# The softmax attention stage of a two-block network: a narrower wait before the differential scores, transposes ahead of the scores in local units, share arithmetic ahead of the maxima

## The reference, cut to what matters

```python
# differential attention, 4 heads, values 128 wide, all 1024+256 keys
s1 = einsum('bqhd,bkhd->bhqk', q1, k1) * SCALE
s2 = einsum('bqhd,bkhd->bhqk', q2, k2) * SCALE
w = softmax(s1) - lam * softmax(s2)
out = einsum('bhqk,bkhe->bqhe', w, v)
# local attention with a sink, 8 heads (2 key heads), values 64 wide,
# a band of 3*128 keys (masked by |q - k| <= 128) and 256 context keys
p = softmax(concat([where(valid, s, -1e30), sink]))[..., :-1]
out = einsum('bhgqk,bkhd->bqhgd', p, v)
```

## Time and profile before

| | us |
|---|---|
| median of 3 runs | 3744.65 (3729.24 to 3747.63) |
| the profiled execution, its time | 3722.19 |
| its span, first to last instruction | 3720.2 |
| TensorE busy, share of the span | 3367.1, 91% |
| mean granted TensorE clock, share of 2.4 GHz | 0.957 |
| pairs of D and L, from the first D's scores to the last D's | 590.28 to 997.44 |

### The profile page before, as it was taken

One profiled execution on the slowest core, in us unless ns is written; L12 is line 12 of the kernel. 1 busy time (PEld: TensorE's weight loads), 2 busy tenths in 40 slices (PEclk: granted clock), 3 DMA queues, 4 the chain that ended last, 5 costly groups with the idle time before them and its releaser, 6 DMA issues. The chain is left out here.

```text
span 3720.2 us, 52552 instructions
## 1 busy us (share of the span) xinstructions
PE 3367.1 (91%) x21754; PEld 2892.5 (78%) x21754; DVE 1628.5 (44%) x2517; ACT 1226.3 (33%) x2230; POOL 260.4 (7%) x332
## 2 busy tenths in 40 slices
PE   7899978999878999997989998887888899999988
PEld 2699976666667999875878995556776799999777
DVE  2306725555555112166536204553555445554343
ACT  3212325555564234223534103442332211111232
POOL 2000000000011000011211100001110000000010
PEclk9899988999988999998999998998999899999999
DMA  9224550000063222233321212001003211111332
GB/s 330 85 83 149 158 181 29 12 12 12 7 214 127 77 73 75 80 115 135 111 51 36 86 44 62 13 1 7 2 2 109 68 45 45 45 45 56 107 126 95
DMA packets 196721, 289.30 MB, mean 78 GB/s; under 512 B 41606, under 2 KB 137670, under 8 KB 194480
## 3 DMA queue, kind: packets, MB, share of 16 engines
q1 hardware_dynamic: 176624, 216.90, 18.1%
q0 software_dynamic: 19904, 69.65, 5.8%
HBM read 217.60 MB, written 68.90 MB: 77 GB/s over the span
## 5 line engine op out<-in xcount | busy, mean ns | idle before, releaser
L115 PE MATMUL p_pb<-p_w_hi,h_hi 128*128 128x416 f32 (+2 forms) x1216 | 425.0, 350 | 6.7 <-DVE p_w_lo L110 6.7
L117 PE MATMUL p_pb<-p_w_hi,h_lo 128*128 128x416 f32 (+2 forms) x1216 | 422.2, 347 | 0.0
L116 PE MATMUL p_pb<-p_w_lo,h_hi 128*128 128x416 f32 (+2 forms) x1216 | 420.0, 345 | 0.0
L115 PE MATMUL fu_pf<-h_hi,fu_w_hi 128*128 128x344 f32 (+1 forms) x1056 | 339.8, 322 | 8.7 <-DVE fu_pf L3426 8.7
L116 PE MATMUL fu_pf<-h_lo,fu_w_hi 128*128 128x344 f32 (+1 forms) x1056 | 340.6, 323 | 0.0
L117 PE MATMUL fu_pf<-h_hi,fu_w_lo 128*128 128x344 f32 (+1 forms) x1056 | 339.2, 321 | 0.0
L115 PEld LDWEIGHTS p_pb<-p_w_hi,h_hi 128*128 128x128 f32 x1216 | 229.2, 189 | 15.7 <-issue 14.4
L116 PEld LDWEIGHTS p_pb<-p_w_lo,h_hi 128*128 128x128 f32 x1216 | 229.4, 189 | 1.9
L117 PEld LDWEIGHTS p_pb<-p_w_hi,h_lo 128*128 128x128 f32 x1216 | 229.2, 188 | 0.6
L115 PEld LDWEIGHTS fu_pf<-h_hi,fu_w_hi 128*128 128x128 f32 x1056 | 200.1, 190 | 9.0 <-DVE fu_pf L3426 9.0
L117 PEld LDWEIGHTS fu_pf<-h_hi,fu_w_lo 128*128 128x128 f32 x1056 | 200.0, 189 | 0.0
(11 more groups left out here) (521 smaller groups left out, 7162.5 us busy)
## 6 DMA issues: line engine op xcount, KB each, us to landing
mod_w<-in_adaln_w SPq DMA_DIRECT2D x12, 2048.0 KB, 16.3
fu_raw<-in_ffn_up SPq DMA_DIRECT2D x88, 256.0 KB, 3.1
fd_raw<-in_ffn_down SPq DMA_DIRECT2D x44, 512.0 KB, 3.6
la_qkv<-p SPq DMA_DIRECT2D x16, 1024.0 KB, 5.1
p<-p_o SPq DMA_DIRECT2D x60, 208.0 KB, 1.9
s_raw<-in_w_in POOLq DMA_DIRECT2D x48, 256.0 KB, 3.5
rT<-p_stage SPq DMA_DIRECT2D x10, 896.0 KB, 4.8
p_raw<-in_ab_w_in POOLq DMA_DIRECT2D x10, 832.0 KB, 6.5
```

The source lines that it names most:

```text
L115: pe.matmul(out, left[0], right[0], start=start, stop=False)
L116: pe.matmul(out, left[0], right[1], start=False, stop=False)
L117: return pe.matmul(out, left[1], right[0], start=False, stop=stop)
```

## The change

Three edits, all in `attention_even`.

1. D's first scores after an L wait for `expd` to reach n - 1, so for L's first exponential alone; a new wait for n stands ahead of D's second scores. The first D, which follows a context unit, keeps its wait for n there.
2. In an L step TensorE transposes the first four blocks of unit u-2 (and waits for its weights) before L's first scores instead of after them. In a D step the order stays.
3. The reciprocal and the share of a `da` or `dac` unit move out of `finish` into `shares`, which VectorE runs for unit u-1 after `take(u-3)` and before `maxima(u)`. It has the wait for both exponentials of u-1 that `finish` has. The combination stays in `finish`.

No instruction of arithmetic is added or removed, and no DMA is touched; SyncE's and GpSimd's programs are the same.

```diff
+                def shares(u):
+                    s, n, h = u % 2, exps_before[u], 4 if units[u][0] == "dac" else 1
+                    dve.wait_ge(expd, n + 2)
+                    dve.reciprocal(r[u % 4][:, 0:2 * h], l[s][:, 0:2 * h]).then_inc(recips, 1)
+                    dve.wait_ge(recips, u + 1)
+                    dve.scalar_tensor_tensor(ratio[:, 0:h], l[s][:, 0:h], g.neglam[:, :], r[u % 4][:, h:2 * h],
+                                             ALU.mult, ALU.mult).then_inc(ratioed, 1)
...
                     if kind in ("da", "dac"):
                         h = 4 if kind == "dac" else 1
                         k = joins_before[u]
-                        dve.reciprocal(r[u % 4][:, 0:2 * h], l[s][:, 0:2 * h]).then_inc(recips, 1)
-                        dve.wait_ge(recips, u + 1)
-                        dve.scalar_tensor_tensor(ratio[:, 0:h], l[s][:, 0:h], g.neglam[:, :], r[u % 4][:, h:2 * h],
-                                                 ALU.mult, ALU.mult).then_inc(ratioed, 1)
                         dve.wait_ge(ratioed, k + 1)
...
                     if u >= 3:
                         take(u - 3)
+                    if 1 <= u <= NU and units[u - 1][0] in ("da", "dac"):
+                        shares(u - 1)
                     if u < NU:
                         maxima(u)
...
                     n = exps_before[u]
+                    near_before = u and kind in ("da", "wa") and units[u - 1][0] in ("da", "wa")
                     if u and part == 0:
-                        pe.wait_ge(expd, n - 1 if kind == "wa" and units[u - 1][0] == "da" else n)
+                        pe.wait_ge(expd, n - 1 if near_before else n)
+                    if near_before and kind == "da" and part == 1:
+                        pe.wait_ge(expd, n)
...
+                    windowed = u < NU and units[u][0] == "wa"
+                    if u < NU and not windowed:
                         score(u, 0)
                     if u >= 2:
                         weighed(u - 2)
                         turn(u - 2, 0)
+                    if windowed:
+                        score(u, 0)
                     if u < NU:
                         score(u, 1)
```

## The result

The changed kernel takes 3687.59 us (median of 4 runs, 3674.2 to 3698.48), the kernel before 3736.94 (4 runs, 3729.21 to 3747.63). The ratio is 0.987, 95% interval 0.9842 to 0.9899: about 49 us, or 1.3%, faster, with 38 to 59 us inside the interval. Eleven more runs of the kernel before, taken later, had a median of 3728.93 us; against those the gain is 41 us. Much of the spread between runs goes with the granted clock: at a mean of 0.951 the kernel before took 3742.62 us and the changed one 3698.48, at 0.953 3739.56 and 3687.24, at 0.954 3733.33 to 3734.34 and 3687.95, so at like clocks 44 to 52 us lie between them. The forecast was 3706 us with a range down to 3694, so the time fell outside it, on the fast side.

The account below looks back on a forecast made before the run. TensorE, busy 91% of the span, was taken as the bound; 31 x 0.76 + 32 x 0.45 + 0.4 = 38.4 us of waits removed from 3744.65 gave 3706 us, range 3700 to 3716, widened to 3694 to 3722.

Parts of the forecast that it names:

- The two waits: TensorE waits for exponentials before each unit's first scores in the attention loop: 0.74 and 0.44 us idle a pair.
- edit 2's leg: TensorE from mask to second scores in a local unit: from 0.99 to 0.54 us, gain 0.45 a pair.
- rival A: Only one of the two waits pays, as chained legs lose one gain: 3720 or 3730 us; chance 12%.
- rival B: On VectorE, the wait in the moved shares holds the maxima: up to 27 us net cost, 3771 us; chance 3%.
- D: As a rival: another releaser stands behind both waits, nothing moves, time within 5 us of 3745; chance 3%.
- Rival C: Granted clock changes: more falls, 1.6 us each (4%), or fewer, with 3704 us (6%); chance 10%.
- The leg to the next D: TensorE from local unit's second scores to the next unit's first: 4.56 to 3.80 us, gain 0.76 a pair.
- the 0.24 us wait: TensorE weight loads before the second transposes wait for ScalarE's first copy; said to go, up to 0.1 us real time.
- The end of the stage: Last transposes wait for the combination; moving shares earlier gains 0.4 us once.
- a case of 6%: Fewer clock falls; the stage's end at full clock gains up to 2 us more, 3704 us; chance 6%.
- TensorE is then the bound: Pair period 11.88 us from legs, 11.91 without waits; so TensorE bounds and the exponential chain just keeps up.
- The modes: TensorE switches between 128-row and 64-row groups: four per local step before and after, so no cost added.

Follow-up runs that it names:

- e2: Kernel before with only the transposes moved ahead of the local unit's first scores; pair period 12.54 us against 13.09.
- e3: Kernel before with only the shares moved ahead of the maxima; pair period 13.09 us, unchanged; idle before the stage's last transposes 0.49 us against 1.29.
- e8: Kernel before with six unused matmuls filling TensorE's wait at the stage's end; last output 22.3 us after the last first scores, 2.8 less.
- e5: Changed kernel with three products of weights and values left out in every local unit; pair period 11.77 us, as in the changed kernel.
- e6: Changed kernel with four repeated products added in every local unit; pair period 12.63 us, 0.86 more.
- e10: Changed kernel with ScalarE's third copy of a local unit cut from two blocks to one, all products kept; pair period 11.73 us.
- e7: Changed kernel with the mask's products ahead of the local unit's band scores, two mode changes fewer; pair period 11.74 us, 3689.37 us, ratio 0.9879.

## Why the prediction was wrong, point by point

**The mechanism was right.** The two waits were TensorE's only idle time, both went, edit 2's leg came out at 0.55 (forecast 0.54) and edit 1 alone at 0.76 (forecast 0.76). In the loop edit 3 was insurance only, worth 0.02 us a pair, and its wait had 0.5 us to spare. Rivals A, B and D did not happen. Rival C came true in its milder form, fewer clock falls: none in the loop, though the transposes stand closer together, and none at the end. The size of the whole was off: the forecast had 38.4 us gained.

**The steps that were mis-sized.** Inside the stage 46.8 us were gained, 8.4 more than forecast:

- The leg to the next D, "from 4.56 to 3.80": it is 3.67. I took the first exponential's read-out at 720.10 as fixed relative to L's second scores. The row of the third copy, directly ahead of the exponential on ScalarE, was in the trace and I had named it in rival A, but as a danger only. It hangs on the transposes before it, and those on the 0.24 us wait that I had noticed and valued at "up to 0.1": that 0.1 belonged in the likeliest value and not only in the bound. 31 pairs x 0.115 = 3.6 us.
- The end of the stage, put at 0.4 us beyond the edit's own 0.45, with up to 2 us more in a case of 6%: in all the end is 4.1 us shorter (25.2 to 21.1), 3.2 more than forecast. The clock that stays up is the greater part: filling that idle time in the kernel before gave 2.8 us by itself. The rest is edit 3, put at 0.4 us, which took 0.80 out of the idle time before the last D's transposes.
- The clock dip in the loop did not recur: 1.6 us. Why, no run shows. Of the four kernels that keep the 0.74 us of idle time before D, the kernel before and e2 had one dip, e3 had one at almost the same place and one in the last pair, and e8 had none; none of the eight kernels with edit 1 had one. That fits fewer dips with less idle time, but four dips in 128 pairs are too few to show it.

**The base and the range.** 18.4 us lie between the forecast and the measured median. 7.7 of them are the kernel before: three runs had a median of 3744.65, four have 3736.94, and the eleven taken later 3728.93. With the last as base the same 38.4 us would have given 3690.5, so the base alone could make the miss of the range. The ratio of the forecast, 38.4 of 3744.65, is 0.9897, and stands just inside the measured interval. The rest is the 8.4 above and some 2 us between medians of four runs. "Three runs of before spread over 18 us, so I add some 6 below" was the weakest line: the high bound of the gain, 44.5 us, already gave 3700, and both the base and the new kernel's median could move by more than those 6 us.

**"TensorE is then the bound"** was the reading of two numbers that agreed, 11.88 and 11.91. The second isn't a floor: 11.77 lies below it. Busy time in the TensorE rows goes by modelled ends, and it also held the 0.12 us by which the wait of the weight loads had delayed the second transposes (0.76 to 0.64), which shows as no idle time of the matmuls. e5 shows that the chain of exponentials still sets the pace, e6 and e10 that TensorE follows within 0.03 to 0.04 us. That the two are nearly even was right. (In rival B, 32 x 0.8 is 25.6 and not 27, the 27 goes with 0.84; nothing hangs on it.)

**The modes.** I added nothing for them, and took the middle of 0.46 and 0.61 for the gap after the mask (measured 0.55, a reduction of 0.44). By the rule of the Trainium skill, page "TensorEngine Tiling (Array Packing)", Key Properties, each change of mode drains the engine. e7 took two changes out of each L step; the one whose price can be read was worth 0.02 us, so a drain that costs 0.2 us or more isn't seen there. The other changes of the step were not priced.

## What to carry to other kernels

When a wait is removed in a loop across engines, follow each in-order queue of that loop once more with the new times: the copy that stood ahead of the exponential moved with the transposes, and its 0.11 us a pair made 3.6 of the 8.4 us missed inside the stage. An idle time of zero doesn't say that the engine is the bound; take some of its work away and see whether the period moves (e5). A short idle time of TensorE at the end of a stage can cost more than itself: behind 1.29 us the clock fell, and filling them gave 2.8 us (e8). See what the granted clock does there before pricing it. And where single runs differ by 25 us, test a gain of 40 by starts inside the stage, pair against pair, take the base from more than three runs, and compare runs at like granted clocks.

## What was not expected of the hardware

- An activation on ScalarE started 0.28 us after the start of a copy of 256 columns (0.38 us long) and 0.17 us after one of 128 columns (0.28 us long), so about 0.1 us before the copy's shown end in both: the queue moves on before the shown end.
- Idle times of 1.28 to 1.40 us before the last D's transposes were each followed by a fall of the granted clock to half in 4 of 4 executions, idle times of 0.49 to 1.09 in none of 6, nor was there a fall where it was filled (e8). Inside the loop, with an idle time of 0.74 us in each pair, the clock fell four times in 128 pairs of four kernels; without it, in none of eight kernels.
- One change between 64-row and 128-row groups of matmuls, taken out of a stretch of the same products, gave 0.02 us (e7).
